# High and low halves of the split weights, interleaved word by word in one buffer

## What is computed

```python
# first block
proj = einsum('bsd,de->bse', rmsnorm(x), w_in)            # 2048 -> 15424 columns
q    = einsum('bsr,re->bse', rmsnorm(q_a), w_q_b)         # 512 -> 3072
kv   = einsum('bsr,re->bse', rmsnorm(c_kv), w_kv_b)       # 512 -> 4096
attn = causal_attention(q, kv) * silu(z_mla)
out  = (sigmoid(g_mla) * (attn @ w_o_mla) + sigmoid(g_conv) * (conv @ w_o_conv)) @ w_out
x    = x + rmsnorm(out)
# second block
proj = rms_norm(concat(meta, x)) @ w_in_2                 # indexer, top-k attention, recurrence
y    = sum(sigmoid(g) * (branch @ w_branch_2))
out  = x + y @ w_out_2
```

## Time and profile before

| | |
|---|---|
| median of 3 runs | 1958.9 us (1958.53 to 1958.91) |
| the profiled execution | 1948.8 us, of which the span is 1947.5 us |
| granted clock of TensorE, mean | 0.998 |
| PE busy | 1933.1 us, 15806 matmuls |
| PEld busy | 1899.4 us, 15806 weight loads |
| DVE busy | 1174.3 us |
| ACT busy | 880.8 us |
| POOL busy | 314.9 us |
| 16 DMA engines, share of the span | about 58% |

### The profile page before, as it was taken

One profiled execution on the slowest core, in us unless ns is written; L12 is line 12 of the kernel. 1 busy time (PEld: TensorE's weight loads), 2 busy tenths in 40 slices (PEclk: granted clock), 3 DMA queues, 4 the chain that ended last, 5 costly groups with the idle time before them and its releaser, 6 DMA issues.

```text
span 1947.5 us, 37136 instructions
## 1 busy us (share of the span) xinstructions
PE 1933.1 (99%) x15806; PEld 1899.4 (98%) x15806; DVE 1174.3 (60%) x1708; ACT 880.8 (45%) x1265; POOL 314.9 (16%) x320
## 2 busy tenths in 40 slices
PE   8999999999999999999999999999999999999999
PEld 8999999999999999999999999999999999999987
DVE  7765665556555455654664665676467776654644
ACT  6444454544444434444445543445443333444443
POOL 3210010202010002300122252040011132110200
PEclk9999999999999999999999999999999999999999
DMA  7565555566666566566565564544564444666564
GB/s 262 155 193 173 164 150 152 166 181 184 186 187 198 189 190 179 183 197 195 192 228 189 179 217 130 143 140 122 161 184 142 133 140 142 174 200 188 185 231 157
DMA packets 175919, 343.79 MB, mean 177 GB/s; under 512 B 10494, under 2 KB 19578, under 8 KB 175226
## 3 DMA queue, kind: packets, MB, share of 16 engines
q1 hardware_dynamic: 174106, 337.16, 57.3%
q10 hardware_dynamic: 1648, 4.26, 0.6%
HBM read 335.09 MB, written 6.29 MB: 175 GB/s over the span
## 4 chain that ended last, share of the span: by engine, by line
PE 94%; DVE 1%; issue 0%; POOL 0%; ACT 0%; POOLq 0%; ACTq 0%; DVEq 0%
PE bank L1284 93%; DVE w_lo L1927 1%; DVE hb L2163 0%; ACT w_hi L1619 0%; DVE scratch L2033 0%; DVE ob_lo L2138 0%; POOL scratch L2523 0%; PE bank L1501 0%; PE bank L1590 0%; PE bank L1440 0%; PE bank L1441 0%; PE bank L1439 0%; PE bank L1591 0%; PE bank L1503 0%; POOL acc_a L2452 0%
## 5 line engine op out<-in xcount | busy, mean ns | idle before, releaser
L1927 DVE TENSOR_TENSOR w_lo<-w_raw,w_hi 128x1024 fp32r<-128x1024 f32 (+2 forms) x644 | 785.9, 1224 | 484.8 <-ACT w_hi L1619 483.3
L1619 ACT ACTIVATE w_hi<-w_raw 128x1024 fp32r<-128x1024 f32 (+2 forms) x644 | 662.9, 1032 | 891.7 <-PE bank L1284 882.9
L1284 PE MATMUL bank<-hb,w_hi 128*128 128x256 f32 x4896 | 865.1, 280 | 1.7 <-DVE hb L1951 1.4
L1284 PEld LDWEIGHTS bank<-hb,w_hi 128*128 128x128 f32 x4896 | 745.9, 188 | 5.0 <-DVE w_lo L1927 3.5
L1284 PE MATMUL bank<-hb,w_lo 128*128 128x256 f32 x2448 | 681.7, 278 | 0.0
L1284 PE MATMUL bank<-ob_hi,w_hi 128*128 128x256 f32 (+1 forms) x2224 | 640.4, 288 | 0.1
L1284 PE MATMUL bank<-ob_lo,w_hi 128*128 128x256 f32 (+1 forms) x2224 | 624.8, 281 | 0.0
L1284 PE MATMUL bank<-ob_hi,w_lo 128*128 128x256 f32 (+1 forms) x2224 | 624.2, 281 | 0.0
L1284 PEld LDWEIGHTS bank<-hb,w_lo 128*128 128x128 f32 x2448 | 459.8, 188 | 0.0
L1284 PEld LDWEIGHTS bank<-ob_hi,w_hi 128*128 128x128 f32 x2224 | 418.1, 188 | 2.5 <-DVE w_lo L1927 0.5
L1284 PEld LDWEIGHTS bank<-ob_lo,w_hi 128*128 128x128 f32 x2224 | 418.1, 188 | 1.6
(11 more groups left out here) (241 smaller groups left out, 1171.4 us busy)
## 6 DMA issues: line engine op xcount, KB each, us to landing
w_raw<-in_w_in SPq DMA_DIRECT2D x436, 512.0 KB, 3.7
w_raw<-in_w_out SPq DMA_DIRECT2D x64, 512.0 KB, 4.4
w_raw<-in_w_o_conv SPq DMA_DIRECT2D x32, 512.0 KB, 4.1
w_raw<-in_w_o_mla SPq DMA_DIRECT2D x32, 512.0 KB, 4.0
w_raw<-in_w_branch SPq DMA_DIRECT2D x32, 512.0 KB, 4.1
w_raw<-in_w_kv_b SPq DMA_DIRECT2D x16, 512.0 KB, 3.7
w_raw<-in_w_q_b SPq DMA_DIRECT2D x16, 384.0 KB, 3.3
arena<-x_kept SPq DMA_DIRECT2D x2, 2048.0 KB, 9.4
```

The lines of the kernel that those rows point to most:

```text
L1284: return nc.tensor.matmul(dst, lhsT, rhs, start=start, stop=stop, skip_group_check=True)
L1619: act(dst, src, ACT.Copy).then_inc(S_("w_hi"), 1)
L1927: tt(low, src, high.bitcast(F32), ALU.subtract).then_inc(S_("w_lo"), 1)
```

## The change

The two buffers of three slots of 1024 words become one of three slots of 1024 pairs of words, the same size. The high half is word 0 of each pair and the low half word 1. Every access to either half then steps by two words, 8 bytes: ACT's write of the high half, DVE's read of the high and write of the low half, PE's weight loads of 128 columns, and PE's moving operand where the weights stream. The raw weights, the transfers, the operands `hb`, `ob_hi` and `ob_lo`, the slots and all the waits are as before. No instruction is added, removed or moved on any engine.

```diff
-        self.whi = sb("w_hi", [P, N_SPLIT, UNIT], F32R)
-        self.wlo = sb("w_lo", [P, N_SPLIT, UNIT], F32R)
+        w = sb("w_split", [P, N_SPLIT, UNIT, 2], F32R)
+        self.whi, self.wlo = w[:, :, :, 0], w[:, :, :, 1]
```

## The result

The changed kernel takes 2105.1 us (median of 4 runs, 2104.5 to 2107.1), the kernel before beside it 1958.7: **+146 us**, a ratio of 1.0759 with a 95% interval of 1.0737 to 1.0780; the two medians alone give 1.0747. The forecast was 2132 in a range of 2005 to 2205.

The account below looks back on a forecast made before the run. PE, busy 99% of the span, was taken as the bound, held by fetching on both ports. Streamed weights +88 and +22 us and weight loads +63 gave +173 on 1958.9: 2132 us, range 2005 to 2205.

Parts of the forecast that it names:

- That PE sets the time and nothing else matters: Whole kernel: PE, busy 99% of the span, sets the time; DVE, ACT and transfers add 0.
- the h = 1 level of the recurrence: DVE operation with all operands at two-word steps: 0.42 us for 256 words against 0.41; basis for 0 extra.
- the predicated copy: DVE operation taking 0.76 us at h = 1, 0.44 at h = 4; upper bound of 1.25 ns more a word.
- Streamed weights, +110 us: Moving operand: 384 matmuls in wout2 gain 229 ns each, +88 us; 192 in kv gain 115 ns, +22 us.
- Weight loads, +63 us: Strided stationary weights: floor 112 to 121 ns, so 12816 matmuls of 256 columns go from 116.1 to 121 ns.
- The lower end of the range: Whole kernel: 2005 us, below the lowest favoured case of 2022, since 63 us may be 46 with floor 120.
- pieces of fixed size: Both PE ports: fetching two or four neighbouring words at a time, so every second word costs 0.89 to 0.90 ns.
- ACT's copy at 1.06 us: ACT's strided write of the high half: unchanged, bounds 0 to +1.3 us, mostly hidden by idle time.
- Loads of `ob_hi` in `wout2` at 188 ns: Stationary loads in the last phase, not strided: length still 188 ns.
- Intervals of 256 columns alike in all stretches: PE matmuls of 256 columns: 121 ns from start to start, the same in every stretch.
- The rival of the fixed line: Both PE ports pick strided words as quickly as neighbours: not slower or a little faster, 1923 to 1981 us; chance 10%.

Follow-up runs that it names:

- apart: Against the kernel before: both halves in one shared buffer, each slot's 1024 high words before its 1024 low ones, nothing strided; 1956.9 us, ratio 0.9999.
- stream_only: Against the kernel before: words interleaved only in kv and wout2, halves apart elsewhere in the same buffer; 2066.3 us, ratio 1.0555.

## Why the prediction was right, point by point

- **That PE sets the time and nothing else matters**: right. DVE's low half stayed at 1254 ns, as the h = 1 level of the recurrence had it; the predicated copy was no guide.
- **Streamed weights, +110 us**: right in size. 106 us between the traces and 109 measured alone. The interval was forecast at 461 ns and is 453, the stage at 180 us and is 178.
- **Weight loads, +63 us**: right in kind, too large. Measured alone it is 40 us, between the traces 50. The length of a load, 197 ns, was right. Mis-sized are the two intervals. Without the gaps at stalls (all intervals under 200 ns) the new one is 120.5 ns, not 121, which is 6 us over 12816 matmuls; the forecast had the floor rise by 9 ns, by the length of a load, and it rose by 7. The old one, 116.1 ns, is 116.6 over the whole trace, another 6 us. The last 10 us, from 50 to 40, aren't in the change: the profiled execution of before had more intervals at 113 ns than that of any other kernel (2304 with `hb`, 1233 in `apart`), and in the traces of `apart` and `stream_only` the old interval is 117.1 and 117.4. Every difference taken from the trace of before is thus too large. I should have given that a place in the sum, having noted that the profile was 10 us fast.
- **The lower end of the range** has a slip: a floor of 120 in place of 121 makes the 63 us 50, not 46, and the end 2009, not 2005. Nothing hangs on it.
- **The step that failed is the reason, not the number.** I took one cause for both ports, pieces of fixed size of which the unused words are lost. For the weight port this fits, with pieces of four words (173 and 233 ns at steps of three and four). For the moving port it doesn't: two neighbours of every four cost as much as two apart (454 and 453 ns for 512 columns), and one of four or eight costs about as much a word as one of two (461 and 431 ns). At a step of two words both readings give 0.89 ns, so the change couldn't tell them apart. That the forecast of the streamed weights came out is in so far luck. Had the change interleaved pairs, pieces of two words would have given a wrong time; had it stepped by four, pieces of four would.
- **ACT's copy at 1.06 us**: wrong, 1.15, inside its bounds, and hidden as argued. **Loads of `ob_hi` in `wout2` at 188 ns**: wrong, 207, hidden too. **Intervals of 256 columns alike in all stretches**: not quite, 120.0 ns in most and 121.7 in some.
- The rival of the fixed line, that nothing slows down, falls for TensorE. A row of matmuls with the moving operand at a step of two words uses two of each four and stands at 453 ns against 227, and weight loads at that step put 117.7 ns under a matmul against 110.6. The Trainium skill, SBUF — State Buffer, section Specifications (TRN2), asks for at least two hits in a 16-byte line for full bandwidth. DVE agrees (1.23 us at a step of two, 2.00 at four) and ACT nearly does (1.12 and 2.00, against 1.06); the moving port disagrees, and there the measurement decides. The Trainium skill, Vector Engine (DVE) Microarchitecture Reference, section Measured stream behaviour on trn2, keeps the full rate for runs of at least two adjacent words; the same 1.23 us at a step of two words contradicts it.

## What to carry to other kernels

Ask of each engine separately what a stride costs it, since the step that is free for VectorE halves TensorE's stream. Where an engine is the bound, compare the pace of each of its streams with the clock; here the one that was slower than the clock had no slack for a stride, and a floor hidden by a few ns showed as soon as it rose by 7. If data must be interleaved for a float32r moving operand, keep runs of four words, and don't start both streams of TensorE at a multiple of 32 words (1985 against 1955 us here). And before a sum is made on one profiled execution, ask whether its paces are those of its fellows.

## What the hardware showed that I had not expected

- The moving port: 0.44 ns a word in runs of four, about 0.9 ns otherwise, for steps of 2, 3, 4 and 8 and for pairs alike.
- The weight port: intervals of 120, 173, 233 ns at steps of 2, 3, 4, and 242 and 222 at 8 and 16, with 256 moving columns; with 128, 110.6 ns in a row and 117.7 at a step of 2.
- A stream at half pace lengthens the weight load beside it from 188 to 207 ns though that load's words are in a row.
- Both streams starting at multiples of 32 words cost 1.5% of the whole kernel (1985 against 1955 us).
- The same matmuls run at 113.3 or at 117.8 ns, and which of the two is fixed for a whole uninterrupted stretch (695 matmuls in 78.8 or in 81.9 us).
